# One layer of convolution, latent attention and experts, then two sparse-attention layers: where the last 31 taps run, and how the first attention weights its values

## The reference, cut to what matters

```
proj = h @ w_in                                  # conv_val, conv_gate, c_q, c_kv, k_rope
u  = conv_val * sigmoid(conv_gate)               # 512 channels
dw = causal_depthwise_conv(u, conv_w, K=31) + conv_b
y_conv = silu(layer_norm(dw))
q, k, v = heads of rms_norm(c_q) @ w_q_b, rms_norm(c_kv) @ w_kv_b   # 8 heads, 96 / 96 / 64 wide
q, k = rms_norm over the head, gains, rotary embedding on the last 32
sc = q k^T * 96**-0.5, masked by chunks of 64 rows
y_attn = softmax(sc) @ v
mixed = concat(y_conv, y_attn) @ w_out ;  x = x + g_a * mixed
... then 32 experts, then two layers of windowed and top-k attention with a dense FFN
```

## Time and profile before

| | |
|---|---|
| median of 3 runs | 2113.76 us (2112.89 to 2116.75) |
| the profiled execution | 2116.16 us |
| its span in the trace | 2114.2 us |
| TensorE's granted clock, mean | 0.968 of full speed |
| PE / DVE / ACT / POOL busy | 92% / 53% / 36% / 9% |
| attention of the first layer | about 193.9 to 259 us of the span |

### The profile page before, as it was taken

The page is one execution under the profiler, slowest core; times in us unless marked ns, Lnnn a source line. Parts: engine busy times, 40 slices in busy tenths (PEclk is TensorE's granted clock), DMA queues, the critical chain, the costliest instruction groups (busy, mean ns, idle before and its releaser), DMA issues. The chain is left out here.

```text
span 2114.2 us, 25239 instructions
## 1 busy us (share of the span) xinstructions
PE 1947.9 (92%) x8762; PEld 1416.8 (67%) x8762; DVE 1127.0 (53%) x1829; ACT 754.6 (36%) x1262; POOL 186.7 (9%) x221
## 2 busy tenths in 40 slices
PE   4997995799999699899999999999989999999997
PEld 2445744566666356686788887865667678888785
DVE  3787734787877668765222223346886622222335
ACT  2024421355554233562233332223257213333222
POOL 1000000232332104001000000000400100000001
PEclk9999997899999899999999999999999999999998
DMA  9162013699996710022033342331002203334130
GB/s 379 60 239 83 15 66 120 214 363 358 355 359 254 265 50 1 21 91 80 21 99 99 93 145 70 114 135 56 1 21 91 60 20 100 99 99 159 60 100 40
DMA packets 148056, 267.15 MB, mean 126 GB/s; under 512 B 11456, under 2 KB 108736, under 8 KB 134784
## 3 DMA queue, kind: packets, MB, share of 16 engines
q1 hardware_dynamic: 141776, 256.29, 34.2%
q0 software_dynamic: 6192, 9.70, 1.4%
HBM read 257.57 MB, written 20.97 MB: 132 GB/s over the span
## 5 line engine op out<-in xcount | busy, mean ns | idle before, releaser
L247 PE MATMUL bank<-ht_hi,gate_up_hi 128*128 128x512 f32 x704 | 274.1, 389 | 2.9 <-ACT arena L1378 2.9
L248 PE MATMUL bank<-ht_lo,gate_up_hi 128*128 128x512 f32 x704 | 273.9, 389 | 0.0
L249 PE MATMUL bank<-ht_hi,gate_up_lo 128*128 128x512 f32 x704 | 273.9, 389 | 0.0
L2341 PE MATMUL bank<-arena 128*128 128x512 f32 (+3 forms) x640 | 193.2, 460 | 8.8 <-ACT arena L1247 5.5
L1706 DVE TENSOR_TENSOR expert_gate_up_lo<-expert_gate_up,expert_gate_up_hi 128x2048 fp32r<-128x2048 f32 x64 | 146.7, 2293 | 56.4 <-ACT expert_gate_up_hi L1163 56.4
L1995 DVE TENSOR_TENSOR arena<-arena,bank 128x512 f32 (+1 forms) x44 | 30.3, 688 | 272.0 <-ACT arena L1266 272.0
L2341 PEld LDWEIGHTS bank<-arena 128*128 128x128 f32 x640 | 113.3, 194 | 83.0 <-issue 65.2
L247 PEld LDWEIGHTS bank<-ht_hi,gate_up_hi 128*128 128x128 f32 x704 | 132.2, 188 | 31.3 <-issue 3.8
L249 PEld LDWEIGHTS bank<-ht_hi,gate_up_lo 128*128 128x128 f32 x704 | 132.2, 188 | 27.4
L248 PEld LDWEIGHTS bank<-ht_lo,gate_up_hi 128*128 128x128 f32 x704 | 132.2, 188 | 27.3
L1163 ACT CAST expert_gate_up_hi<-expert_gate_up 128x2048 fp32r<-128x2048 f32 x64 | 121.6, 1901 | 70.4 <-PE bank L249 70.3
(11 more groups left out here) (356 smaller groups left out, 3473.1 us busy)
## 6 DMA issues: line engine op xcount, KB each, us to landing
gate_up_whole<-w_gu SPq DMA_DIRECT2D x88, 512.0 KB, 5.1
expert_gate_up<-w_gate_e SPq DMA_DIRECT2D x32, 1024.0 KB, 7.0
expert_gate_up<-w_up_e SPq DMA_DIRECT2D x32, 1024.0 KB, 9.8
arena<-w_down_e SPq DMA_DIRECT2D x32, 1024.0 KB, 5.3
down_whole<-w_down SPq DMA_DIRECT2D x44, 512.0 KB, 3.5
arena<-w_ada SPq DMA_DIRECT2D x5, 4096.0 KB, 20.5
arena<-w_in SPq DMA_DIRECT2D x4, 2048.0 KB, 16.4
w_o_whole<-w_o SPq DMA_DIRECT2D x2, 4096.0 KB, 13.5
```

What stands on the lines that cost most here:

```text
L247: pe.matmul(ps, xh, wh, start=start, stop=False)
L248: pe.matmul(ps, xh, wl, start=False, stop=False)
L249: return pe.matmul(ps, xl, wh, start=False, stop=stop)
L2341: ins = pe.matmul(ps[:, 0:b - a], HT[:, c, t * P:(t + 1) * P], w_in2[j][:, c], start=c == 0, stop=c == C8 - 1)
```

## The change

Three edits, all in the first layer's mixing.

1. DVE keeps the taps of groups 0 to 2 (`DVE_TAPS` = 93). POOL computes group 3 after its two latent scales: one `tensor_scalar`, then for each of 30 taps a `tensor_scalar` into one of two buffers and a `tensor_tensor` that adds it, each behind a wait for the one before. DVE's 6 remaining taps come one a step in steps 0 to 5.
2. `FILLERS` and their products are gone.
3. Values are the weights now: for a pair of heads, V (128x64) is loaded into one or the other half of the array's columns, the moving operand is 128 columns of transposed probabilities, and the output lies transposed already (head dimension on the partitions). `values` runs once per pair, two steps later in the order. The row sums' reciprocals are spread over partitions by 8 products with the identity (`spread_sums`, with a bank of its own), ACT copies them (`take_sums`), and DVE multiplies straight into `mixT` (`take_o`). The transposes and copies of `oT` are gone, and so is `O`.

```diff
-FILLERS = 2
+DVE_TAPS = (MC - 1) * TAPS
+SUMS_AT = {NH * t + NH + 3: t for t in range(T)}
@@ POOL, behind the latent scales
+            u1.evacuated(pool, ("taps",))
+            u1.evacuated(pool, ("val", MC - 1))
+            pool.wait_ge(s_small, SMALL)
+            own.link(pool.tensor_scalar(DW[:, MC - 1], U[:, MC - 1, 0:S], conv_w[:, MC - 1, 0:1], conv_b[:, MC - 1:MC], ALU.mult, ALU.add))
+            for k in range(1, TAPS):
+                tap = POOL_TAP[:, k % 2]
+                own.link(pool.tensor_scalar(tap, U[:, MC - 1, k:k + S], conv_w[:, MC - 1, k:k + 1], None, ALU.mult))
+                ins = pool.tensor_tensor(DW[:, MC - 1], DW[:, MC - 1], tap, ALU.add)
+                if k < TAPS - 1:
+                    own.link(ins)
+                else:
+                    ins.then_inc(s_conv, 1)
@@ ACT
+            def take_sums(t):
+                ps = u1.read(act, ("sums", t))
+                if t >= 2:
+                    u1.evacuated(act, ("o", t - 2))
+                u1.free(act.copy(SUMS[:, t % 2], ps[:]), ("sums", t))
...
-            for j in range(4):
-                ps = u1.read(act, ("oT", j))
-                u1.free(act.copy(mixT[:, 4 + j], ps[:]), ("oT", j))
+            take_sums(T - 1)
@@ DVE
+            def invert(t):
+                u1.evacuated(dve, ("s", t, NH - 1))
+                dve.reciprocal(rl[:, t], lsum[:, t]).then_inc(s_inv, 1)
             def take_o(t):
-                u1.evacuated(dve, ("s", t, NH - 1))
-                own.link(dve.reciprocal(rl[:, t], lsum[:, t]))
+                u1.evacuated(dve, ("sums", t))
                 ps = u1.read(dve, ("o", t))
...
-                for _ in range((0, 1, 2, 2)[min(n // NH, T - 1)]):
-                    if k < MC * TAPS:
-                        conv(k // TAPS, k % TAPS)
-                        k += 1
+                if k < DVE_TAPS:
+                    conv(k // TAPS, k % TAPS)
+                    k += 1
@@ PE
-                for _ in range(FILLERS):
-                    pe.matmul(ps[:], ident_b, chunk_mask.unsqueeze(1).broadcast_to([P, 4, P]), start=True, stop=True)
...
             def values(n):
                 t, h = divmod(n, NH)
-                u1.evacuated(pe, ("pT", t, h))
+                for p in range(2):
+                    u1.evacuated(pe, ("pT", t, h + p))
                 for k in range(t + 1):
-                    ins = pe.matmul(ps[:, h * VD:(h + 1) * VD], PT[:, n % 3, k * P:(k + 1) * P], V[:, k, h * VD:(h + 1) * VD],
-                                    start=k == 0, stop=k == t)
+                    for p in range(2):
+                        ins = pe.matmul(ps[VD * p:VD * (p + 1), h // 2 * P:(h // 2 + 1) * P], V[:, k, (h + p) * VD:(h + p + 1) * VD],
+                                        PT[:, (n + p) % 3, k * P:(k + 1) * P], start=k == 0, stop=k == t)
+            def spread_sums(t):
+                pe.wait_ge(s_inv, t + 1)
+                ps = u1.begin(pe, ("sums", t))
+                for h in range(NH):
+                    ins = pe.matmul(ps[VD * (h % 2):VD * (h % 2 + 1), h // 2 * P:(h // 2 + 1) * P], rl[:, t, h:h + 1].broadcast_to([P, VD]), ident,
+                                    start=True, stop=True)
+                u1.full(ins, ("sums", t))
-            for n in range(T * NH + 3):
+            for n in range(T * NH + 4):
...
-                if n >= 3:
-                    values(n - 3)
-            for j in range(4):
-                ...
-                turn(("oT", j), [O[:, t, j * P:(j + 1) * P] for t in range(T)])
+                if n >= 4 and n % 2 == 0 and n < T * NH + 4:
+                    values(n - 4)
+                if n in SUMS_AT:
+                    spread_sums(SUMS_AT[n])
```

More of the change, by code:

```diff
@@ L154, in plan_first @@
         b.take(("o", t), bank=6 + t % 2)
-        for h in range(NH):
-            b.take(("s", t, h), among=6)
-            b.take(("pT", t, h), among=6)
+    for n in range(T * NH + 4):
+        if n < T * NH:
+            b.take(("s", n // NH, n % NH), among=6)
+        if 2 <= n < T * NH + 2:
+            b.take(("pT", (n - 2) // NH, (n - 2) % NH), among=6)
+        if n in SUMS_AT:
+            b.take(("sums", SUMS_AT[n]), among=6)
     b.next = 0
-    for j in range(4):
-        b.take(("oT", j))
     b.take(("mean",))
@@ L425, in build @@
         rope_t = KT.rearrange("p h n -> p (h n)")[:, 0:4 * T * NH * 16].rearrange("p (k n) -> p k n", k=4)
-        O = at(H0, T, NH * VD)
+        SUMS = at(H0, 2, 512)
+        POOL_TAP = at(H0 + T * NH * QK, 2, S)
         mixT = HT
@@ L643, in build @@
         s_pv = sem("values_weighted")
-        s_prob = sem("probabilities")
+        s_inv = sem("sums_inverted")
         s_x1 = sem("x1_done")
@@ L743, in weighted @@
             t, h = divmod(n, NH)
-            if h == NH - 1:
+            if h >= NH - 2:
                 u1.read(eng, ("o", t))
             else:
-                eng.wait_ge(s_pv, t * (NH - 1) + h + 1)
+                eng.wait_ge(s_pv, t * (NH // 2 - 1) + h // 2 + 1)
         def weighted2(eng, n, l):
@@ L797, in load_down @@
                 sp.dma_start(ring_d[s], i["w_down_e"][0][bass.ds(n, 1)].rearrange("a (p c) n -> (a p) c n", c=2)).then_inc(s_dn[s], 16)
-            u1.read(sp, ("oT", 0))
+            u1.read(sp, ("sums", T - 1))
             load_gate_up(2, 2)
@@ L1123, in _ @@
                         take_pt(n - 3)
+                    if n - 1 in SUMS_AT:
+                        take_sums(SUMS_AT[n - 1])
                     act.wait_ge(s_negmax, n + 1)
@@ L2178, in _ @@
                     turn_p(n - 2)
-                if n >= 3:
-                    values(n - 3)
-            for j in range(4):
-                for t in range(T):
-                    u1.evacuated(pe, ("o", t))
-                turn(("oT", j), [O[:, t, j * P:(j + 1) * P] for t in range(T)])
+                if n >= 4 and n % 2 == 0 and n < T * NH + 4:
+                    values(n - 4)
+                if n in SUMS_AT:
+                    spread_sums(SUMS_AT[n])
             ps = u1.begin(pe, ("mean",))
@@ L2190, in _ @@
             pe.wait_ge(s_wout, 64)
-            for j in range(4):
-                u1.evacuated(pe, ("oT", j))
             def mix(t, half, ms):
                 ps = u1.begin(pe, ("mix", t, half)) if ms[0] else bank[u1.b.where[("mix", t, half)][0]]
+                if ms[0] == MC:
+                    u1.evacuated(pe, ("o", t))
                 for m in ms:
```

13 lines of the change are left out of this document (8 added, 5 removed).

## The result

| | before | after |
|---|---|---|
| median | 2115.34 us (2112.89 to 2123.3, 5 runs) | 2124.55 us (2122.71 to 2127.17, 5 runs) |
| ratio | | 1.0041, 95% interval 1.0027 to 1.0054 |
| profiled execution / its span | 2116.16 / 2114.2 us | 2127.17 / 2125.4 us |
| keys' transposes start (K) | 188.74 | 200.31 |
| scores of steps 0, 8, 16, 24, 31 start | 194.32, 203.52, 216.54, 234.43, 252.07 | 206.69, 216.96, 231.91, 247.23, 264.27 |

The change costs 9.2 us of the medians. K is 11.6 us later, and M - K, from the keys' transposes to the mean, is 2.35 us shorter. Behind M the two profiled executions differ by 2 us more; the change touches nothing there.

What follows compares the result with a forecast made beforehand. DVE's chain of squares, scaling and rotation was taken to bound the time before the attention, PE its last tile. Taps 25, attention -8, clock +3 make +20 on 2116.16: 2136, as a median 2134; range 2107 to 2147.

Steps and rivals of the forecast that it cites:

- POOL's taps: DVE's chain ahead of the attention: 44 instructions wait for POOL's reads, 25 us in all, bounds 0 to 38.
- The means that were to show it: Sign in DVE's squares, scaling and rotation: mean instruction times of 1.4 to 1.7 us instead of 0.96 and 0.69.
- its length less 0.21: DVE's wait behind a POOL instruction, from rows at 804 us: 1.07 us behind two-operand, 0.47 behind one-operand.
- its first rival: DVE's chain: POOL nearly free for DVE, contention 2 us instead of 25, attention -8 to -11; 2106 us, chance 14%.
- POOL's end: POOL's group of taps ends near 213 us, about when DVE's rotation ends; the mean needs it beyond 250.
- The attention: Attention loop about 4 us shorter and its tail about 4, together -8 us; bounds +5 to -22.
- The cycle of two steps: Attention's last tile: PT's three buffers and paired values close a cycle of 4.65 us per two heads, 2.3 a head.
- Its reason: Attention loop: PT has three buffers and values come in pairs, so a cycle of two steps closes at 4.65 us.
- The halves side by side: Values on PE: two array halves run together, 0.86 us a pair, 1.05 with 0.2 for changing over twice.
- The rival in which the halves run one after the other: Values on PE: a pair costs 1.9 us, the cycle 5.5, attention +3, total +30; 2144 us, chance 12%.
- The clock: PE in the attention: two stretches of a few us at 1.2 GHz, 1.5 us dearer each, +3; bounds 0 to +12.
- That the whole of PE's relief counts: Attention: the cycle of two steps is looser than drawn, -22 + 25 + 0 = +3; 2117 us, chance 12%.

Runs made afterwards that it cites:

- p2: Changed kernel with POOL's 60 instructions behind the first all one-operand multiplies, the last group's convolution not computed; 2116.09 us (1 run).
- p3: Changed kernel with POOL's 60 instructions behind the first all two-operand sums, the last group's convolution not computed; 2140.53 us (1 run).
- e1: Changed kernel without POOL's block, the last group's taps back on DVE in the loop; 2112.87 us, 0.9981 of the kernel before.
- e5: Changed kernel with a fourth buffer in PT and nothing else; 2127.08 us (1 run).
- e5b: Changed kernel with a fourth buffer in PT and each pair of values one step later on PE; 2115.49 us (1 run).
- e3b: Changed kernel with the extra products put back in row tiles 0 and 1 only; 2127.67 us, 1.0049 of the kernel before.
- e7: e5b with POOL waiting for DVE's rotation and taking only the group's last 14 taps, DVE the other 17; 2101.07 us, 0.9916 of the kernel before.

## Why the prediction was right or wrong

Forecast 2134 us, 20 more than before; measured 2124.55, 9.2 more. The sign and the mechanism stand (POOL's reads stretch DVE's chain ahead of the attention, and the attention gives back less), the size is less than half. By the steps:

- **POOL's taps, +25 forecast, +11.6 measured. This is the term that failed.** Piecewise: to the first squares 1.2 (2.4 forecast), squares 2.1 up to the start of the scaling at 173.22 (6), scaling and rotation 8.3 (16.8). The squares themselves took 3.6 us more, and the 1.93 us wait for PE behind them, which the forecast let swallow little, took up 1.5 of it. The means that were to show it (1.4 to 1.7 us) came out at 1.38 for L1497's counterpart, 1.10 for L1511's and 1.04 for L1521's. Two errors stand in it and work against each other. The one-operand instruction of 128x512 was put at 0.69 us by the slope of a cast; it takes 1.56 alone. And "its length less 0.21", true of a two-operand instruction against another, was carried over to the one-operand form, which holds DVE up hardly at all: 0.07 us per DVE instruction where 0.47 was forecast (p2). The two-operand form was forecast at 1.28 us and 1.07 behind each, and measured 1.26 and 0.90 on the rotation's products (p3), but 0.65 over all 44. So the pace of the taps, 3.0 us and not 2.1, also met DVE with fewer two-operand instructions. The forecast had the missing possibility in the wrong place: in its first rival, "the one-operand half of its work does not hold it", but only together with a two-operand half that falls into gaps.
- **POOL's end** was forecast at 213 us and is 237.8, still far from the mean.
- **The attention, -8 forecast with +3 for the clock; measured -2.35 together.** From K on: to the scores of step 0 +0.8, row tile 0 +1.07, tile 1 +1.93, tile 2 -2.57, tile 3 to step 31 -0.6, from there to the mean -2.98. The forecast had nothing up to the end of tile 0, then -1, -1.5, -2.8 with 1.5 of waits to be added, and -4. Without POOL's taps the same attention gives 4.5 us (e1), near the 5 that the forecast had with the clock: part of the shortfall belongs to the taps. The cycle of two steps came out as drawn (4.65 forecast, 4.71 to 4.95 measured, as was PE's wait for ACT's copy ahead of the values), but a step of the last tile before was not 2.7 us: (252.07 - 234.43) / 7 = 2.52. The one step whose rows I added up had the whole work in it, and products overlap at their ends.
- **Its reason was wrong**: a fourth buffer alone changes nothing (e5), so it is not `PT`'s three buffers that close the cycle; with the values one step later behind four buffers it opens (e5b), which points to the order of values and scores on PE and of exponential and copy on ACT. The price was right because the chain of durations is the same; a reader who had acted on the reason would have added a buffer for nothing.
- **The halves side by side**: forecast 1.05 a pair, measured 1.02 to 1.09, and 0.1 for each changing over beside it, 1.2 in all. The rival in which the halves run one after the other, 1.9 a pair, did not come.
- **The clock, +3**: forecast as a stretch or two at 1.2 GHz. It was one long stretch in row tiles 0 and 1, worth 1.9 us (e3b). I had put it into the loop as a whole, from a forecast of 45 busy us of 61 for PE; it was 54.9 of 65.6, with the slow products in it.
- **A smaller misreading**: DVE stood still in a third place behind the latent scales, 1.21 us for PE ahead of 136.71, before and after alike. It changes no term.
- **That the whole of PE's relief counts** was a rival, rightly put low for this order; with the values a step later it does count: -14.6 us of M - K (e5b against before).

## What to carry to other kernels

Two-operand work of POOL (1.26 us an instruction) cost a DVE chain mostly of two-operand instructions 0.65 us for each, and 0.9 for a two-operand product of the same size; one-operand work cost 0.07 and 0.14, writes nothing of such a product but 0.5 to 0.8 us of a one-operand copy or scaling: give POOL its two-operand work when DVE has slack, not when DVE's chain is what the others wait for. Beside the head chain all 31 taps of the group cost 11.6 us; 14 of them inside the attention cost 0.5 at most.

When a loop over three engines runs longer than its busiest engine, write down which instruction stands behind which on each engine before giving it another buffer; here a fourth buffer alone took nothing out, and moving the values by one step with that buffer in place 12 us.

A term that is carried from one form of an instruction to another needs bounds of its own.

## What the runs showed that was not expected

- POOL's `tensor_scalar` of 128x512 that only multiplies takes 1.56 us, longer than its `tensor_tensor` of the same size, 1.26. The chain's first, which multiplies and adds the bias, takes half of that, near the 0.69 forecast for both. The start of its input isn't the cause: in p2 the first product that only multiplies has the same input from the same column and takes about 1.8 us (134.02 to 135.79). In e7 the chain's first only multiplies, into a third place (`POOL_SUM`), and takes 1.59 us (188.53) while DVE has no two-operand work. That speaks for the missing second operation rather than the place of the output, but no run changes one of them alone; it stays open.

```profile
133.43 0.76 POOL L949 TENSOR_SCALAR arena<-arena 128x512 f32<-128x512 f32 x1
134.29 1.79 POOL L952 TENSOR_SCALAR arena<-arena 128x512 f32<-128x512 f32 x1
136.16 1.26 POOL L953 TENSOR_TENSOR arena<-arena 128x512 f32<-128x512 f32 x1
```

- Such a one-operand POOL instruction delays a DVE instruction that starts near its own start (0.41 us at 154.45) and not one that starts 1.7 us into it (152.14).
- PE's clock was 0.54 over 18 us, and full over the same 18 us once each step had two more products of 512 bf16 columns, whose result is overwritten. The busy share was 83% either way, for 71 products in the first case and 110 in the second: a busy share at the lower clock says little about how much work there is.
